# Four extra matmuls with unused results in front of twenty of attention's transpose groups

## The chip, the cores and the metric

The kernel runs on one core of one Trainium2 chip. The metric is the device time of one execution in microseconds (us), from the first to the last instruction with what lies around it. Lower is better. In this document PE is TensorE, DVE is VectorE, ACT is ScalarE, POOL is GpSimd, SP is SyncE.

## What is computed

The reference is a two-layer decoder trunk over 512 tokens of width 1024. Layer 0 is an RWKV-7 mixer, layer 1 is native sparse attention; each stands between two half-step SwiGLU blocks. The change lies in the attention of layer 1, which has 16 heads of width 64 in 4 groups of 4:

```python
lc = jnp.einsum('bqghd,bngd->bqghn', qc, k_cmp) * scale
p_cmp = masked_softmax(lc, ...)                     # 31 compressed keys
o_cmp = jnp.einsum('bqghn,bngd->bqghd', p_cmp, v_cmp)
...
ls = jnp.einsum('bqghd,bqgkd->bqghk', qrc, kg) * scale
p_sel = masked_softmax(ls, causal)
o_sel = jnp.einsum('bqghk,bqgkd->bqghd', p_sel, vg)
...
lw = jnp.einsum('bqghd,bkgd->bqghk', qrc, kw) * scale
p_win = masked_softmax(lw, ...)
o_win = jnp.einsum('bqghk,bkgd->bqghd', p_win, vw)
return gc[..., 0:1] * o_cmp + gc[..., 1:2] * o_sel + gc[..., 2:3] * o_win
```

With 512 tokens, 8 blocks and 16 wanted, all blocks are selected, and the window covers all tokens: both large branches are causal attention over all keys, with different keys and values.

## The kernel before

Attention is a list of 44 steps, `STEPS`, which is run twice (`i` is 0 and 1, two groups of heads in each run, called passes here). Each head has one step `cmp` (the compressed branch, all 512 queries) and four steps `main` (128 queries each, `t` is 0 to 3; the scores of both large branches against the first `128 (t+1)` keys). After every two heads a step `turn` transposes their output; it stands behind `cmp` and `main` `t=0` of the next head. By the number `u` in a pass, the steps `cmp` are 0, 5, 10, 16, 21, 27, 32 and 38, the steps `turn` 12, 23, 34 and 43.

PE works through the list in program order, in three parts for each step, which are staggered: `scores` of step u+1, then `turn(u)` (the method that transposes the probabilities of step u, one 128x128 block at a time, into PSUM banks 4 and 5), then `weigh` of step u-1 (transposed probabilities times values). In the profile `scores` are L2410 (`cmp`) and L2421 to L2423 (`main`), the transposes are L2443 (`cmp`), L2449 (`main`) and L2439 (a step `turn`), and `weigh` is L2468 (`cmp`) and L2475 (`main`; a matmul there shows as two records). DVE takes the negated row maxima (L2592, L2595, L2598), ACT the exponentials (L2506, L2512), and both copy the transposed blocks out of banks 4 and 5 (DVE L2612, ACT L2526 and L2529; for a step `turn` ACT L2524 and then DVE L2607). The methods wait through `at(engine, i, name, u)`, which waits until the event `name` of step u has been counted; `copied_a` and `copied_v` are the copies by ACT and DVE. POOL splits the keys and queries of the next group into a rounded part and a rest meanwhile (L2549 to L2561).

Inputs of the new matmuls are `q2[g]` (queries of a group, 128 columns of the first head as weights) and `khi[g][:, 0]` (512 rounded keys as the moving operand), both already in SBUF.

Of the kernel before, what the change touches and what calls it, by code (L numbers as in the profile page):

```python
# [13 lines left out]
P = 128  # L14
# [679 lines left out]
def recurrence(core, tag, rkv, lora, yhi, ylo):  # L694

    nc, ins = core.nc, core.ins
    with ExitStack() as ctx:
# [109 lines left out]
        def _(pe):  # L807
# [187 lines left out]
            def step(p):  # L995
# [7 lines left out]
                if ahead:  # L1003
                    rates(p + 1)
                product(p, 1)
                turn(p, 0)
                update(p, 1)
                chain(p - 1, 2)
                if ahead:
                    key_norm(p + 1)  # L1010
                product(p, 2)
                turn(p, 1)
                chain(p - 1, 3)
                update(p, 2)
# [5 lines left out]
                chain(p - 1, 4)  # L1020
                update(p, 3)
                turn(p, 2)
                chain(p - 1, 5)
                product(p, 4)
# [724 lines left out]
class SharedKv(Heads):  # L1749
# [129 lines left out]
    def turn(self, pe, n):  # L1879
        u, c = self.turned[n], self.c  # L1880
        pe.wait_ge(self.s["xt"], u + 1)
        for t in range(NT):
            mm = self.core.nc.tensor.transpose(self.p_c[:, t * P:(t + 1) * P], self.xt[:, u % 4, t * P:(t + 1) * P], self.core.ident[:])
        mm.then_inc(c["turned"], 1)
# [422 lines left out]
def attention_steps():  # L2307
    steps, turn = [], None
    for group in range(2):
        for pair in range(2):  # L2310
            for head in range(2):
                steps.append(("cmp", group, pair, head, 0))
                steps += [("main", group, pair, head, t) for t in range(NT)][0:1]
                if turn and head == 0:
                    steps.append(turn)
                steps += [("main", group, pair, head, t) for t in range(1, NT)]
            turn = ("turn", group, pair, 0, 0)
    return steps + [turn]


STEPS = attention_steps()
# [14 lines left out]
class Attend:  # L2336
# [62 lines left out]
    def scores(self, pe, i, u):  # L2399
# [23 lines left out]
            mm = nc.tensor.matmul(bank[:, at0 + b, t * P:n], self.ident16[:], self.causal16[:], start=False, stop=True)  # L2423
        mm.then_inc(s["scores"], 1)

    def turn(self, pe, i, u):
        nc, s, bank = self.nc, self.s, self.bank
        kind, g, pair, head, t = STEPS[u]
        self.at(pe, i, "copied_v", u - 1)
        self.at(pe, i, "copied_a", u - 1)  # L2430
        if i == 0 and u == 0:
            pe.wait_ge(self.heads.s["ln"], ND)
        if i == 0 and u == 1:
            pe.wait_ge(self.heads.s["t2"], ND - 1)
        if kind == "turn":
            last = max(w for w in range(U) if STEPS[w] == ("main", g, pair, 1, NT - 1))
            self.at(pe, i, "o", last)
            for t in range(NT):
                mm = nc.tensor.transpose(bank[:, 4, t * P:(t + 1) * P], self.osb[:, pair, t], self.core.ident[:])  # L2439
        elif kind == "cmp":  # L2440
            self.at(pe, i, "probs", u)
            for t in range(NT):
                mm = nc.tensor.transpose(bank[0:N_CMP, 4, t * P:(t + 1) * P], self.probs[:, u % 2, 0, t * N_CMP:(t + 1) * N_CMP],  # L2443
                                         self.core.ident[:])
        else:
            for b in range(2):
                self.at(pe, i, "probs_sel" if b == 0 else "probs", u)
                for j in range(t + 1):
                    mm = nc.tensor.transpose(bank[:, 4 + b, j * P:(j + 1) * P], self.probs[:, u % 2, b, j * P:(j + 1) * P],  # L2449
                                             self.core.ident[:])  # L2450
        mm.then_inc(s["turned"], 1)
# [302 lines left out]
```

## Time and profile before

| | |
|---|---|
| median of 3 runs | 2480.82 us (2479.68 to 2481.47) |
| the profiled execution, its own time | 2479.42 us |
| its span, first to last instruction | 2477.6 us |
| PE busy | 2356.4 us, 95% of the span |
| mean granted clock of TensorE | 0.974 |
| attention on PE | about 1801 to 2058 us of the span |

A granted clock of 1.00 is 2.4 GHz, 0.50 is 1.2 GHz. Matmuls on PE overlap each other, so what a matmul costs in a dense row of them is read from the distance between two starts and not from its duration: in the rows below the number at the start of a timeline row is its start in us from the beginning of the span, the next its length in us, and a bracket at its end is the time that the engine stood idle before it with what released it.

### The profile page before, as it was taken

How to read it: one execution, taken by the hardware profiler on the slowest of the kernel's cores; microseconds unless marked ns; L12 is line 12 of the kernel's file. 1: busy time of each engine (PE TensorE's matmuls, PEld its weight loads, DVE VectorE, ACT ScalarE, POOL GpSimd, SP SyncE). 2: the span in 40 equal slices, each digit the busy share in tenths (PEclk: the TensorE clock that was granted, in tenths of full speed). 3: DMA queues.
4: the chain of work that ended last, by engine and by line, in shares of the span. 5: the costliest groups of instructions: out<-in, count | busy, mean ns of one | idle time of the engine just before them, and what ended most of it. 6: DMA issues, size and time to landing. Idle time of an engine off the chain costs nothing. (4 is left out here: it accounts for less than half of the span.)

```text
span 2477.6 us, 43846 instructions
## 1 busy us (share of the span) xinstructions
PE 2356.4 (95%) x17558; PEld 1926.6 (78%) x17558; DVE 1536.2 (62%) x2159; ACT 647.8 (26%) x1250; POOL 499.2 (20%) x334
## 2 busy tenths in 40 slices
PE   7999998997988789999999999999999999999999
PEld 6888886784766568888888888888778887888887
DVE  7656467846777556655575565647766666655654
ACT  3101014534555521010023310102544552200001
POOL 3212031002122132121230121213221102212211
PEclk9999998998999989999999999999988999999999
DMA  4333332431111033323265242333300002232322
GB/s 139 102 90 97 102 93 81 143 110 57 30 30 27 3 94 93 102 85 110 79 175 158 86 118 85 101 99 97 86 1 14 14 2 85 85 110 85 104 87 72
DMA packets 371394, 206.54 MB, mean 83 GB/s; under 512 B 18400, under 2 KB 360352, under 8 KB 371232
## 3 DMA queue, kind: packets, MB, share of 16 engines
q1 hardware_dynamic: 364752, 192.11, 27.1%
q10 hardware_dynamic: 6480, 12.13, 1.4%
q8 instruction: 119, 1.95, 0.3%
q14 instruction: 43, 0.35, 0.0%
HBM read 192.61 MB, written 11.60 MB: 82 GB/s over the span
## 5 line engine op out<-in xcount | busy, mean ns | idle before, releaser
L158 PE MATMUL bank_b<-hhi_b,w_hi_b 128*128 128x512 f32 x872 | 345.6, 396 | 0.0
L160 PE MATMUL bank_b<-hhi_b,w_lo_b 128*128 128x512 f32 x872 | 339.5, 389 | 0.0
L159 PE MATMUL bank_b<-hlo_b,w_hi_b 128*128 128x512 f32 x872 | 339.3, 389 | 0.0
L151 DVE TENSOR_TENSOR w_lo_b<-w_raw,w_hi_b 128x1024 fp32r<-128x1024 f32 (+1 forms) x165 | 289.7, 1756 | 5.7
L158 PE MATMUL bank_a<-hhi_a,w_hi_a 128*128 128x512 f32 x480 | 189.2, 394 | 7.7 <-DVE hlo_a L573 7.7
L159 PEld LDWEIGHTS bank_b<-hlo_b,w_hi_b 128*128 128x128 f32 x872 | 163.7, 188 | 37.0 <-issue 3.4
L158 PEld LDWEIGHTS bank_b<-hhi_b,w_hi_b 128*128 128x128 f32 x872 | 163.7, 188 | 36.6 <-issue 3.4
L160 PEld LDWEIGHTS bank_b<-hhi_b,w_lo_b 128*128 128x128 f32 x872 | 163.7, 188 | 34.4
L159 PE MATMUL bank_a<-hlo_a,w_hi_a 128*128 128x512 f32 x480 | 188.4, 392 | 0.0
L160 PE MATMUL bank_a<-hhi_a,w_lo_a 128*128 128x512 f32 x480 | 188.2, 392 | 0.0
L479 POOL TENSOR_TENSOR act_b<-gated_b,usc_b 128x512 f32<-128x512 f32 x44 | 63.9, 1451 | 485.1 <-ACT gated_b L458 485.1
L151 DVE TENSOR_TENSOR w_lo_a<-w_raw,w_hi_a 128x1024 fp32r<-128x1024 f32 (+2 forms) x96 | 158.3, 1648 | 3.3
L458 ACT ACTIVATE gated_b<-gsc_b 128x512 f32<-128x512 f32 x44 | 27.9, 634 | 495.1 <-DVE gsc_b L369 495.1
L369 DVE TENSOR_TENSOR gsc_b<-bank_b,rstd_b 128x512 f32<-128x512 f32 x44 | 30.4, 691 | 193.4 <-PE bank_b L160 193.4
L158 PE MATMUL bank_b<-ahi_b,w_hi_b 128*128 128x512 f32 x352 | 137.4, 390 | 1.2 <-DVE x_res L381 1.2
L158 PE MATMUL bank_c<-hhi_c,w_hi_c 128*128 128x512 f32 x352 | 137.3, 390 | 0.0
L159 PE MATMUL bank_b<-alo_b,w_hi_b 128*128 128x512 f32 x352 | 136.9, 389 | 0.0
L160 PE MATMUL bank_c<-hhi_c,w_lo_c 128*128 128x512 f32 x352 | 136.9, 389 | 0.0
L160 PE MATMUL bank_b<-ahi_b,w_lo_b 128*128 128x512 f32 x352 | 136.9, 389 | 0.0
L159 PE MATMUL bank_c<-hlo_c,w_hi_c 128*128 128x512 f32 x352 | 136.9, 389 | 0.0
L151 DVE TENSOR_TENSOR w_lo_c<-w_raw,w_hi_c 128x1024 fp32r<-128x1024 f32 (+1 forms) x76 | 134.8, 1774 | 2.6
L149 DVE CAST w_hi_b<-w_raw 128x1024 fp32r<-128x1024 f32 (+1 forms) x165 | 112.5, 682 | 4.3 <-PEq L2195 4.3
(373 smaller groups left out, 4914.5 us busy)
## 6 DMA issues: line engine op xcount, KB each, us to landing
w_raw<-in_ffn_w_gate_dram SPq DMA_DIRECT2D x88, 512.0 KB, 3.8
w_raw<-in_ffn_w_up_dram SPq DMA_DIRECT2D x88, 512.0 KB, 3.8
w_raw<-in_ffn_w_down_dram SPq DMA_DIRECT2D x64, 512.0 KB, 3.7
w_raw<-in_ffn_w_down_dram SPq DMA_DIRECT2D x32, 384.0 KB, 3.3
w_raw<-in_rw_w_rkv_dram SPq DMA_DIRECT2D x24, 512.0 KB, 3.8
w_raw<-in_kv_w_dram SPq DMA_DIRECT2D x12, 512.0 KB, 4.8
w_raw<-in_rw_w_o_dram SPq DMA_DIRECT2D x8, 512.0 KB, 5.0
w_raw<-in_nsa_w_q_dram SPq DMA_DIRECT2D x8, 512.0 KB, 3.8
```

Source lines behind the costliest of these rows:

```text
L149: nc.vector.tensor_copy(hi, raw).then_inc(s["w_hi"], 1)
L151: nc.vector.tensor_tensor(lo, raw, fp(hi), ALU.subtract).then_inc(s["w_ready"], 1)
L158: nc.tensor.matmul(out, whi, hi, start=first, stop=False)
L159: nc.tensor.matmul(out, whi, lo, start=False, stop=False)
L160: return nc.tensor.matmul(out, wlo, hi, start=False, stop=last)
L369: V.tensor_tensor(region.gsc[:, j], bank[:, j], region.rstd[:], ALU.mult).then_inc(s["gate"], 1)
L458: A(region.gated[:], region.gsc[:, j], ACT.Silu).then_inc(s["silu"], 1)
L479: G_.tensor_tensor(region.act32[:], region.gated[:], region.usc[:, j], ALU.mult).then_inc(s["act32"], 1)
```

## The change

In front of the transposes of step u, a new method issues four matmuls into PSUM bank 5: for every step `cmp` but the first of a pass, and for each step `main` that stands right behind a step `turn`. Nothing reads their results; the next transposes into bank 5 overwrite them. Ahead of them PE waits for the ACT copy out of bank 5 of the step before (or, behind a turn, of the one before that).

```diff
+    def keep_clock(self, pe, i, u):
+
+        kind, g = STEPS[u][:2]
+        if u and (kind == "cmp" or kind == "main" and STEPS[u - 1][0] == "turn"):
+            self.at(pe, i, "copied_a", u - 1 if kind == "cmp" else u - 2)
+            for _ in range(4):
+                self.nc.tensor.matmul(self.bank[:, 5], self.q2[g][:, 0, 0:P], self.khi[g][:, 0], start=True, stop=True)
+
     def turn(self, pe, i, u):
         nc, s, bank = self.nc, self.s, self.bank
         kind, g, pair, head, t = STEPS[u]
+        self.keep_clock(pe, i, u)
         self.at(pe, i, "copied_v", u - 1)
         self.at(pe, i, "copied_a", u - 1)
```

In each pass the places are the steps `cmp` 5, 10, 16, 21, 27, 32, 38 and the steps `main` 13, 24, 35: ten places, twenty in both passes, 80 matmuls of 128x512.

The first of them on PE, step 5 of the first pass, as a piece of the difference in PE's program order (lines of the kernel after are 9 higher from the method on):

```order
 L2422 MATMUL bank_b<-klo_b,q_b 128x128
 L2423 MATMUL bank_b<-causal_b,ident_b 128x128
-L2443 MATMUL bank_b<-ident,probs_b 31x128 x4
-L2475 MATMUL bank_b<-vv_b,pt_b 128x64 x8
+L2432 MATMUL bank_b<-khi_b,q_b 128x512 x4
+L2452 MATMUL bank_b<-ident,probs_b 31x128 x4
+L2484 MATMUL bank_b<-vv_b,pt_b 128x64 x8
 L2421 MATMUL bank_b<-khi_b,q_b 128x256
 L2422 MATMUL bank_b<-klo_b,q_b 128x256
```

The four new matmuls (L2432) stand between the scores of step 6 and the transposes of step 5; what follows keeps its order.

A place behind a turn, step 13 of the first pass, on PE as well:

```order
 L2422 MATMUL bank_b<-klo_b,q_b 128x384
 L2423 MATMUL bank_b<-causal_b,ident_b 128x128
-L2449 MATMUL bank_b<-ident,probs_b 128x128 x4
+L2432 MATMUL bank_b<-khi_b,q_b 128x512 x4
+L2458 MATMUL bank_b<-ident,probs_b 128x128 x4
 L2421 MATMUL bank_b<-khi_b,q_b 128x512
 L2422 MATMUL bank_b<-klo_b,q_b 128x512
```

Here the four stand between the scores of step 14 and the transposes of step 13, for which PE waits until the output of the turn has been copied out of bank 4.

## Rows read from the trace of the kernel before

**Rows 1.** The page: the span, and busy time of the engines.

```profile
span 2477.6 us, 43846 instructions
PE 2356.4 (95%) x17558; PEld 1926.6 (78%) x17558; DVE 1536.2 (62%) x2159; ACT 647.8 (26%) x1250; POOL 499.2 (20%) x334
```

**Rows 2.** Windows over attention: stretch, its length, busy time of engines, granted clock.

```profile
1801.00:1814.50 13.50, 10.44 (x65) 7.33 (x64) 10.89 (x27) 6.43 (x26) 9.08 (x7) 1.00 0.00 1
1814.50:1838.40 23.90, 23.55 (x103) 21.09 (x103) 10.09 (x36) 7.85 (x30) 3.74 (x4) 0.50 0.00 1
1838.40:1886.20 47.80, 43.53 (x352) 38.79 (x352) 33.63 (x111) 26.12 (x96) 6.49 (x6) 1.00 0.08 18
1886.20:1903.30 17.10, 17.10 (x76) 14.70 (x75) 6.72 (x23) 5.48 (x24) 4.41 (x5) 0.50 0.01 1
1903.30:1940.80 37.50, 34.03 (x278) 30.62 (x277) 23.77 (x82) 18.83 (x66) 0.00 (x0) 1.00 0.04 9
1940.80:1951.00 10.20, 8.90 (x41) 7.38 (x40) 5.08 (x18) 4.51 (x21) 7.40 (x7) 0.50 0.23 51
1951.00:2060.30 109.30, 99.57 (x801) 88.30 (x801) 72.85 (x254) 58.84 (x216) 3.48 (x4) 1.00 0.00 1
2060.30:2067.10 6.80, 5.33 (x13) 4.17 (x14) 6.66 (x8) 0.00 (x0) 0.00 (x0) 0.50 0.55 159
```

**Rows 3.** Timeline of PE: transposes of steps 3, 5 and 10, first pass.

```profile
1814.85 1.51 PE L2449 MATMUL bank_b<-ident,probs_b 128*128 128x128 f32 x6 [2.54 <-ACT pt_b L2529]
...
1825.06 1.06 PE L2443 MATMUL bank_b<-ident,probs_b 128*31 128x128 f32 x4
...
1844.23 0.60 PE L2443 MATMUL bank_b<-ident,probs_b 128*31 128x128 f32 x4
```

**Rows 4.** Timeline of PE, second pass: transposes of steps 3 and 10.

```profile
1952.21 0.83 PE L2449 MATMUL bank_b<-ident,probs_b 128*128 128x128 f32 x6
...
1971.04 0.60 PE L2443 MATMUL bank_b<-ident,probs_b 128*31 128x128 f32 x4
```

**Rows 5.** Timeline of PE, first pass: steps 25, 26 and 32.

```profile
1881.64 0.84 PE L2449 MATMUL bank_b<-ident,probs_b 128*128 128x128 f32 x6 [0.32 <-issue]
...
1885.33 1.15 PE L2449 MATMUL bank_b<-ident,probs_b 128*128 128x128 f32 x8 [1.01 <-ACT pt_b L2529]
...
1909.04 0.60 PE L2443 MATMUL bank_b<-ident,probs_b 128*31 128x128 f32 x4
```

**Rows 6.** Timeline of PE, second pass: steps 25 and 32.

```profile
2008.46 0.84 PE L2449 MATMUL bank_b<-ident,probs_b 128*128 128x128 f32 x6 [0.32 <-issue]
...
2027.04 0.60 PE L2443 MATMUL bank_b<-ident,probs_b 128*31 128x128 f32 x4
```

**Rows 7.** Timeline of PE: a dense row of 128x512 matmuls, full clock.

```profile
1800.12 0.40 PE L158 MATMUL bank_b<-hhi_b,w_hi_b 128*128 128x512 f32 x1
1800.35 0.39 PE L159 MATMUL bank_b<-hlo_b,w_hi_b 128*128 128x512 f32 x1
```

**Rows 8.** Timeline of PE: the same kind of matmul at half clock.

```profile
2063.22 0.63 PE L158 MATMUL bank_c<-ohi_b,w_hi_c 128*128 128x512 f32 x1
2063.64 0.63 PE L159 MATMUL bank_c<-olo_b,w_hi_c 128*128 128x512 f32 x1
```

**Rows 9.** Timeline of PE: 128x512 scores with the operands of the new matmuls.

```profile
2048.54 0.47 PE L2421 MATMUL bank_b<-khi_b,q_b 128*128 128x512 f32 x1
2048.86 0.40 PE L2422 MATMUL bank_b<-klo_b,q_b 128*128 128x512 f32 x1
```

**Rows 10.** Timeline of PE: the wait behind a turn (step 12, second pass).

```profile
1977.05 0.23 PE L2423 MATMUL bank_b<-causal_b,ident_b 128*128 128x128 bf16 x1
1978.34 0.44 PE L2449 MATMUL bank_b<-ident,probs_b 128*128 128x128 f32 x2 [1.06 <-DVE olo_b L2607]
```

**Rows 11.** Timeline of ACT and PE, second pass: ACT's copy of step 15, transposes of step 16.

```profile
1985.11 0.57 ACT L2529 ACTIVATE pt_b<-bank_b 128x512 f32<-128x512 f32 x1
...
1985.88 0.60 PE L2443 MATMUL bank_b<-ident,probs_b 128*31 128x128 f32 x4
```

## The prediction

> **What bounds the kernel now.** I read four views, from coarse to fine. The page comes first: PE is busy for 2356.4 us of the span of 2477.6 us, 95% [rows 1], so what is added on PE in a dense part of the program costs time unless it stands in a gap. The windows over attention are second, cut where the granted clock changes. They show four stretches at 0.50, 1.2 GHz: 23.9, 17.1, 10.2 and 6.8 us long, and 1.00, 2.4 GHz, between them [rows 2]. The first three lie in attention, 51.2 us together; the fourth lies behind it, in the output projection. At half clock PE is busy for 23.55 us of 23.9 and 17.10 of 17.1, while DVE falls from 33.63 us in 47.8 (0.70) to 10.09 in 23.9 (0.42) [rows 2]: there nothing but PE sets the pace. At full clock PE is busy for 99.57 us of 109.3 [rows 2]; the rest is gaps.
>
> The timeline is third; it prices the half clock. The list of steps is the same in both passes, so the same pieces can be compared. From the transposes of step 3 to those of step 10 the first pass takes 1844.23 - 1814.85 = 29.38 us [rows 3], the second, at full clock, 1971.04 - 1952.21 = 18.83 us [rows 4]. The first stretch thus costs 10.55 us for its 23.9 us, 0.44 us for each us at half clock. From step 25 to step 32 it is 1909.04 - 1881.64 = 27.40 us [rows 5] against 2027.04 - 2008.46 = 18.58 us [rows 6], 8.82 us more, of which 1.01 us is a wait for ACT ahead of the transposes of step 26 [rows 5] and 7.8 us the second stretch, 0.46 for each us. The third has no clean counterpart; by 0.45 for each us it costs 10.2 x 0.45 = 4.6 us. All that can be won in attention is therefore 10.6 + 7.8 + 4.6 = 23 us.
>
> **What stands before a fall, and where the clock comes back.** The first fall, at 1814.5, comes at the end of an idle time of 2.54 us ahead of the transposes of step 3 [rows 3], the second, at 1886.2, behind the 1.01 us of rows 5. In the second pass the transposes of step 25 stand at the same place without a fall [rows 2, 6]. The first two stretches end at the same place of the list: 1838.4 is 5.8 us ahead of step 10, 1903.3 is 5.7 us ahead of step 32 [rows 2, 3, 5]. By the program order that is behind the scores of a step with `t=3`, the row of wide matmuls (four of 128x512) that is the densest thing attention has. The clock falls where PE has little to do and returns where wide matmuls stand close together.
>
> **The change, part by part.** It adds 80 matmuls of 128x512 in twenty groups of four, and one wait ahead of each group. DVE, ACT, POOL and SP execute what they did.
>
> Price of a group. A dense row of such matmuls goes at 0.23 us each at full clock [rows 7] and 0.42 us at half clock [rows 8], so a group takes 0.92 us or 1.68 us. With the very operands of the new matmuls, the first one of a pair of scores takes 0.32 us to the next [rows 9], but that one follows a narrow matmul with other weights, so I use it only as the upper bound, 1.28 us a group. The lower bound is nothing, where a gap of PE hides the group. The Trainium skill, page "TensorE: Matmul & The Clock Gate", section "Back-to-back issue gap", gives some 131 ns for each matmul of 512 columns in a sustained stream of loads and matmuls, against about 216 ns for a single one; the row of this case, 230 ns, agrees with the second. By the page's first figure a group would cost 0.52 us.
>
> The six groups behind a turn. PE has issued the scores at 1977.05 and then stands idle for 1.06 us, until DVE's copy L2607 is done, at 1978.34 [rows 10]. The new matmuls wait for a copy two steps back, which is old by then, so they fit in: 0.92 against 1.06 us. Cost 0 (if a group takes 1.28 us, 6 x 0.22 = 1.3 us). Without that cover they would cost 5.5 us.
>
> The fourteen groups in front of a `cmp` step. There the transposes follow the scores with no idle time, both at step 10 [rows 4] and at step 16 [rows 11]: no cover, and what follows on PE moves back by the whole group. The wait that comes with them is free: ACT's copy out of bank 5 ends at 1985.11 + 0.57 = 1985.68, and PE comes to this place at 1985.88 [rows 11]. Queued behind it are the transposes of the step, for which ACT and DVE wait, and these then run later by the same 0.92 us; since PE is the slower side, no gap elsewhere shrinks that I can name. Thirteen at full clock, 12.0 us, and the one of step 5 in the first pass, at half clock, 1.7 us: 13.7 us.
>
> What they give back. The first fall comes at 1814.5, 10.6 us before the first group could run (step 5, at 1825.06) [rows 2, 3]. Nothing in the change prevents it. But the group of step 5 is as dense as the scores of a `t=3` step, and it follows the scores of step 6. I expect the clock back right behind it, at about 1825.1 + 1.7 + 1.5 = 1828.3 instead of 1838.4. That is 10 us fewer at half clock, 10 x 0.44 = 4.4 us. The second fall needs the thin place of steps 25 and 26 and the wait in it, which came once in the two passes. The group ahead of step 24 brings dense work near it, but it stands in front of the scores of 25 and not in the thin place itself, so it is no sure cure. In the likeliest case the second stretch does not open: 7.8 us. If it opens, the group of step 27 ends it some 7 us later, and 10 x 0.45 = 4.5 us are won, with a second group at half clock (0.8 us more). The third stretch opens at the passage between the passes, where steps 39 to 43 and 0 to 4 have no new matmuls; I leave it and the fourth as they are, a gain of 0.
>
> **The sum.** 13.7 - 4.4 - 7.8 = +1.5 us. Against the profiled execution's own 2479.42 us that makes 2480.9; this execution lies 1.4 us under the median of the runs, so on the median it is 2480.8 + 1.5 = 2482.3 us.
>
> **The rivals.**
>
> *The second stretch opens all the same, or one elsewhere instead.* For it: the groups move all that follows by several us, and thin places at `t=2` and `t=3` of each head stay. Cost 13.7 + 0.8 - 4.4 - 4.5 = +5.6 us, 2486.4; with the third stretch longer by 3 to 7 us, up to 2490.
>
> *The clock does not care.* The groups stand at the wrong places or are too short, each stretch ends where it did, and the whole price is left: 14 x 0.92 = 12.9 us, and at half clock for three or four of them 0.8 us more each, +15 to +16 us, 2496. Against it: the stretches do end behind a dense row of about this size. That the change does not do what it says is this case.
>
> *The other side: all later falls stay away.* The mechanism is the passage between the passes: if its fall at 1940.8 is as marginal as that of step 26, a small shift is enough, and 4.6 us come on top, with about 3 us more if the fourth stretch (6.8 us at 0.45) goes too. It decides if both happen: 1.5 - 4.6 - 3.1 = -6.2 us, 2474.6; with the third alone -3.1 us, 2477.7, not to be told from no change. Against it: no new matmul stands between step 38 and step 5 of the next pass, and PE has 1.3 us of idle time in the 10.2 us of the third stretch [rows 2].
>
> *The groups are cheaper than a dense row.* If a group lets DVE and ACT catch up and so closes gaps of PE behind it, or its four matmuls follow each other more closely than 0.23 us because they share their weights, the price halves to 6.9 us: 1.5 - 6.8 = -5.3 us, 2475.5. The rows have no gap for it beside the one behind a turn and a third of a us in front of a `t=2` step [rows 5, 6]. The page's 131 ns would come to about this.
>
> **How the numbers follow.** A measurement of this kernel tells 0.2%, 5.0 us, from no change. Chances: the likeliest case 0.42, with its own range 2478 to 2486 (price of a group up to 1.28 us adds 14 x 0.36 = 5 us; the third stretch gone takes 4.6). The second stretch or another opens, 0.30, of which two thirds end above 2485.8. The clock does not care, 0.08. All later falls stay away or shorten, 0.13, of which half is under 2475.9. Cheaper groups, 0.07. Faster: 0.06 + 0.05 and a little of the first case, 0.14. Slower: 0.20 + 0.08 and 0.04 of the first, 0.32. Within 0.2%: 0.54. The range reaches from the two faster cases to the top of the second rival, 2474 to 2491; outside it are the case in which the clock does not care and the ends of the others.
>
> **What the profile after would show.** The new line L2432 with 80 matmuls, start to start 0.23 us. Idle time of PE ahead of the transposes behind a turn falls from 1.06 to about 0.15 us. In the second pass, from the transposes of step 25 to those of step 32, 18.58 us become 20.4, since the groups of steps 27 and 32 lie between. A first fall at 1814.5 as before, its end at about 1828. The stretch round step 26 gone or at most some 7 us. The third and the fourth about 10 and 7 us. The prediction is wrong if the first stretch still lasts 24 us, if new stretches at half clock open, or if a group takes clearly more or less than 0.92 us.

## The result, and the profile after

| | before | after |
|---|---|---|
| median of 11 runs each | 2479.68 us (2475.72 to 2484.68) | 2485.22 us (2480.98 to 2489.11) |
| the profiled execution, its own time | 2479.42 us | 2484.16 us |
| its span | 2477.6 us | 2482.4 us |

The ratio is 1.0021, with a 95% interval of 1.0011 to 1.0030: the change makes the kernel some 5.5 us slower. Single runs of either kernel lie up to 9 us apart, more than the effect, so it takes medians to see it. One run of the kernel before, among those set beside the later experiments, took 4132.46 us at a mean granted clock of 0.666; no ratio and no range below counts it.

The windows of the kernel after, cut where its granted clock changes, with the columns of [rows 2]:

```profile
1814.60:1828.30 13.70, 13.33 (x59) 12.52 (x60) 6.25 (x19) 4.91 (x20) 3.21 (x4) 0.50 0.00 1
1828.30:1886.30 58.00, 55.63 (x427) 48.19 (x426) 38.12 (x127) 30.14 (x111) 7.08 (x6) 1.00 0.06 15
1886.30:1893.20 6.90, 6.90 (x31) 6.24 (x31) 2.91 (x8) 2.31 (x10) 3.81 (x5) 0.51 0.00 1
1893.20:1940.90 47.70, 43.55 (x337) 37.84 (x336) 29.05 (x102) 23.17 (x85) 0.00 (x0) 1.00 0.06 13
1940.90:1951.20 10.30, 10.26 (x41) 7.88 (x42) 5.50 (x15) 3.87 (x15) 8.51 (x8) 0.50 0.11 24
...
2063.80:2070.60 6.80, 3.06 (x7) 2.51 (x8) 5.66 (x7) 0.23 (x1) 0.00 (x0) 0.50 0.26 77
```

The first stretch at half clock begins where it did, at 1814.6, and lasts 13.7 us instead of 23.9. The second still opens, and lasts 6.9 us instead of 17.1. The third and fourth are as long as before. In attention 51.2 us at half clock have become 30.9.

Where the first stretch ends, PE's timeline of the kernel after shows the group of step 5 at half clock and the scores behind it back at full clock:

```profile
1825.06 0.33 PE L2423 MATMUL bank_b<-causal_b,ident_b 128*128 128x128 bf16 x1
1825.15 2.06 PE L2432 MATMUL bank_b<-khi_b,q_b 128*128 128x512 f32 x4
1827.01 1.05 PE L2452 MATMUL bank_b<-ident,probs_b 128*31 128x128 f32 x4
...
1829.98 0.28 PE L2422 MATMUL bank_b<-klo_b,q_b 128*128 128x256 f32 x1
```

And step 26, the wait in the thin place, with the group of step 27 behind it:

```profile
1884.84 1.06 PE L2458 MATMUL bank_b<-ident,probs_b 128*128 128x128 f32 x8 [1.02 <-ACT pt_b L2538]
...
1888.73 2.06 PE L2432 MATMUL bank_b<-khi_b,q_b 128*128 128x512 f32 x4
1890.59 1.05 PE L2452 MATMUL bank_b<-ident,probs_b 128*31 128x128 f32 x4
```

The wait for ACT is there as before, 1.02 us against 1.01 [rows 5]. A group takes 1827.01 - 1825.15 = 1.86 us at half clock. At full clock, in the second pass, first in front of a `cmp` step and then behind a turn:

```profile
1970.87 0.23 PE L2423 MATMUL bank_b<-causal_b,ident_b 128*128 128x128 bf16 x1
1970.91 1.17 PE L2432 MATMUL bank_b<-khi_b,q_b 128*128 128x512 f32 x4
1971.92 0.60 PE L2452 MATMUL bank_b<-ident,probs_b 128*31 128x128 f32 x4
...
1977.92 0.23 PE L2423 MATMUL bank_b<-causal_b,ident_b 128*128 128x128 bf16 x1
1977.96 1.17 PE L2432 MATMUL bank_b<-khi_b,q_b 128*128 128x512 f32 x4
1979.21 0.66 PE L2458 MATMUL bank_b<-ident,probs_b 128*128 128x128 f32 x4
```

From the last row of the scores (1970.87) to the transposes it is 1.05 us, where the kernel before had 0.07 (1970.97 to 1971.04), so a group costs 0.98 us. Counted in the same way it costs 1.83 us at half clock: 1.95 us (1825.06 to 1827.01), where the kernel before had 0.12 (1824.94 to 1825.06). Behind the turn no idle time is left in brackets, where [rows 10] had 1.06 us, and the transposes come as soon as they did, 1.29 us behind the last row of the scores in both kernels.

The account of attention can be made from the same anchors as before: the transposes of steps 3, 10, 25 and 32 of the first pass, of step 42, and of step 3 of the second pass.

```profile
1814.97 1.51 PE L2458 MATMUL bank_b<-ident,probs_b 128*128 128x128 f32 x6 [3.11 <-ACT pt_b L2538]
...
1841.76 0.60 PE L2452 MATMUL bank_b<-ident,probs_b 128*31 128x128 f32 x4
...
1881.13 0.84 PE L2458 MATMUL bank_b<-ident,probs_b 128*128 128x128 f32 x6 [0.32 <-issue]
...
1905.95 0.60 PE L2452 MATMUL bank_b<-ident,probs_b 128*31 128x128 f32 x4
...
1931.96 1.06 PE L2458 MATMUL bank_b<-ident,probs_b 128*128 128x128 f32 x8 [0.79 <-issue]
...
1951.05 0.89 PE L2458 MATMUL bank_b<-ident,probs_b 128*128 128x128 f32 x6
```

Steps 3 to 10 take 26.79 us instead of 29.38 [rows 3], with two groups in them (1.83 + 0.98), so 5.4 us came back. Steps 25 to 32 take 24.82 us instead of 27.40 [rows 5], again with two groups: 5.4 us. Together that is 10.8 us for 20.4 us less at half clock, 0.53 for each us. The price is 12 x 0.98 + 2 x 1.83 = 15.4 us. The difference is +4.6 us. From step 42 to step 3 of the second pass it is 19.09 us; before it was 18.13 us, 1.0 us more at an equally long stretch, with no group in it. Why is not shown. These are the anchors of the kernel before in that piece, the last turn and step 0 of the next pass between them:

```profile
1934.08 0.63 PE L2449 MATMUL bank_b<-ident,probs_b 128*128 128x128 f32 x4 [0.79 <-issue]
...
1939.00 0.63 PE L2439 MATMUL bank_b<-ident,lora_lg 128*128 128x128 f32 x4 [0.79 <-DVE lora_lg L2648]
...
1943.06 1.03 PE L2443 MATMUL bank_b<-ident,probs_b 128*31 128x128 f32 x4 [1.30 <-ACT probs_b L2506]
```

That makes +5.6 us in attention. The projection behind it gives 1.0 us back, since fewer of its matmuls fall into the fourth stretch (they start at 2067.5 and the clock returns at 2070.6; before it was 2061.8 and 2067.1). The span is 4.8 us longer.

### The profile page after: what moved, and what is told of

Read it like the earlier page. It is cut to its first block and busy times, and to the rows that moved or that the text cites. A ratio compares the mean times of both kernels' runs of the same rounds, so it can differ in the third digit from the quotient of the medians.

```text
span 2482.4 us, 44006 instructions
## 1 busy us (share of the span) xinstructions
PE 2367.8 (95%) x17638; PEld 1933.0 (78%) x17638; DVE 1538.9 (62%) x2159; ACT 649.2 (26%) x1250; POOL 499.0 (20%) x334
## 3 DMA queue, kind: packets, MB, share of 16 engines
q8 instruction: 119, 1.95, 0.3%
```

## The experiments

All kernels below compute the same output as the two compared; only the matmuls with unused results differ. Times are medians, each beside the median of the kernel before from runs taken together with it.

**Which groups do what: only those of steps 5 and 27, first pass.**

```diff
-        if u and (kind == "cmp" or kind == "main" and STEPS[u - 1][0] == "turn"):
+        if i == 0 and u in (5, 27):
```

> Only the groups ahead of steps 5 and 27 of the first pass are left, 8 new matmuls. Theory (these two alone shorten the half clock, the others only cost): both stretches end as in the changed kernel, 13.7 and 6.8 us long; won 10.2 x 0.44 + 10.2 x 0.45 = 9.1 us, paid 2 x 1.82 = 3.6 us: 5.5 us under the kernel before, ratio about 0.9978. Rival (the other groups have a part in it, by what they add to the activity of PE between): one of the two stretches is long again, and the time is within 2 us of the kernel before.

Measured: 2473.38 us against 2479.3, ratio 0.9974 (0.9963 to 0.9985), 5.9 us faster. The windows of its trace:

```profile
1815.10:1828.80 13.70, 12.84 (x57) 12.04 (x58) 6.70 (x22) 5.19 (x21) 3.69 (x4) 0.50 0.01 1
...
1883.30:1890.10 6.80, 6.80 (x31) 6.14 (x30) 2.18 (x8) 2.61 (x13) 4.68 (x5) 0.50 0.01 4
```

The two stretches are those of the changed kernel, 13.7 and 6.8 us. Two of the twenty groups are enough for all the shortening; the other eighteen are not needed for it.

**Only the six groups behind a turn.**

```diff
-        if u and (kind == "cmp" or kind == "main" and STEPS[u - 1][0] == "turn"):
+        if u and kind == "main" and STEPS[u - 1][0] == "turn":
```

> Only the six groups behind a turn. Theory (they lie in a wait and change no stretch): time as before within 1 us, the four stretches 23.9, 17.1, 10.2 and 6.8 us, PE's idle time behind a turn about 0.1 us instead of 1.06. Rival A (they cost, by what they delay on other engines): 3 to 6 us slower. Rival B (the group ahead of step 24 has part in shortening the second stretch): that stretch under 14 us and the time 2 us or more under before.

Measured: 2479.63 us against 2479.3, ratio 0.9998 (0.9989 to 1.0008). They cost nothing and bring nothing. In the trace the first two stretches are 23.9 and 17.1 us, the third is 13.6 and not 10.2 us:

```profile
1811.90:1835.80 23.90, 22.69 (x102) 20.65 (x102) 11.18 (x38) 8.72 (x34) 3.92 (x5) 0.50 0.00 1
...
1883.60:1900.70 17.10, 17.10 (x78) 15.42 (x76) 7.49 (x25) 5.78 (x24) 5.00 (x5) 0.50 0.00 0
...
1938.20:1951.80 13.60, 12.71 (x53) 10.08 (x53) 6.20 (x21) 5.49 (x24) 9.22 (x9) 0.50 0.22 55
```

**Only the fourteen groups in front of `cmp` steps.**

```diff
-        if u and (kind == "cmp" or kind == "main" and STEPS[u - 1][0] == "turn"):
+        if u and kind == "cmp":
```

> Only the fourteen groups ahead of cmp steps. Theory: 12 at full clock x 0.98 = 11.8 us and 2 at half clock x 1.82 = 3.6 us, against 9.1 us won: 6 us slower than before in attention, 5 to 6 us in the whole, the same as the changed kernel within 1 us. Rival (the groups behind turns have a part in cost or gain): differs from the changed kernel by 2 us or more.

Measured: 2483.87 us against 2478.86, ratio 1.0024 (1.0013 to 1.0035): 5.0 us slower, as the changed kernel within 1 us. The whole effect is in these fourteen. In the trace the first two stretches are 13.7 and 6.8 us, as in the changed kernel.

**Only the seven groups in front of `cmp` steps of the second pass**, where the clock was whole.

```diff
-        if u and (kind == "cmp" or kind == "main" and STEPS[u - 1][0] == "turn"):
+        if i == 1 and u and kind == "cmp":
```

> Only the seven groups ahead of cmp steps of the second pass, where the clock is whole before the change. Theory (they bring nothing there and each costs 0.98 us): 6.9 us over before, less up to 1 us if the fourth stretch covers less of the projection. Rival (part of the price is got back, since PE's other waits shrink): 3 us or less over before.

Measured: 2485.09 us against 2479.52, ratio 1.0021 (1.0011 to 1.0030), 5.6 us slower. That is 0.80 us a group, against 0.98 less what the fourth stretch gives back (7 x 0.98 - 1.0 = 5.9 us). These seven alone cost as much as the whole change costs on balance. Its profiled run, the fastest of nine, had a second stretch of 3.4 us where nothing had been changed ahead of it: how long a stretch lasts varies from run to run.

**What about a group brings the clock back: narrow matmuls.** As the kernel with two groups, with eight matmuls of 64 columns in each.

```diff
-        if u and (kind == "cmp" or kind == "main" and STEPS[u - 1][0] == "turn"):
+        if i == 0 and u in (5, 27):
-            for _ in range(4):
-                self.nc.tensor.matmul(self.bank[:, 5], self.q2[g][:, 0, 0:P], self.khi[g][:, 0], start=True, stop=True)
+            for _ in range(8):
+                self.nc.tensor.matmul(self.bank[:, 5, 0:64], self.q2[g][:, 0, 0:P], self.khi[g][:, 0, 0:64], start=True, stop=True)
```

> As two_groups, but with eight matmuls of 64 columns in each group instead of four of 512: at half clock a group takes about the same time (8 x 0.22 = 1.8 us), PE is as busy, but 512 columns pass instead of 2048. Theory (the columns count): the stretches are as long as before the change, 23.9 and 17.1 us, and the time is 3 to 4 us over before. Rival (that PE is busy counts): the stretches end as in two_groups, and the time is 5.5 us under before.

Measured: 2483.02 us against 2479.3, ratio 1.0016 (1.0008 to 1.0025), 3.7 us slower. Its timeline and its windows:

```profile
1828.24 1.90 PE L2432 MATMUL bank_b<-khi_b,q_b 128*128 128x64 f32 x8
1829.95 1.04 PE L2452 MATMUL bank_b<-ident,probs_b 128*31 128x128 f32 x4
```

```profile
1816.60:1843.90 27.30, 25.84 (x114) 23.28 (x115) 11.06 (x40) 9.09 (x34) 2.97 (x3) 0.50 0.00 1
...
1891.70:1908.80 17.10, 17.10 (x77) 15.22 (x77) 6.97 (x23) 5.06 (x20) 3.85 (x5) 0.50 0.00 0
```

A narrow group keeps PE busy for 1829.95 - 1828.24 = 1.71 us, nearly as long as a wide one (1.86 us). The stretches last 27.3 and 17.1 us, where the kernel before had 23.9 and 17.1. The price is paid, 2 x 1.71 = 3.4 us, and nothing comes back. So the time for which PE counts as busy does not decide: behind four matmuls of 512 columns the clock came back, behind eight of 64 columns, with twice as many weight loads, it did not.

**Four matmuls in the wait of step 26 alone.** From here on all edits are against the kernel before, and the count, the bank and the step whose use of the bank must be over come from a table. `turn` calls the new method first, as in the changed kernel; that line is left out below.

```diff
+    def keep_clock(self, pe, i, u):
+
+        count, bank, before = {(0, 26): (4, 7, 23)}.get((i, u), (0, 0, 0))
+        g = STEPS[u][1] if STEPS[u][0] != "turn" else 0
+        if count:
+            self.at(pe, i, "o", before)
+            if STEPS[u][0] == "turn":
+                pe.wait_ge(self.s["split"], 15)
+            for _ in range(count):
+                self.nc.tensor.matmul(self.bank[:, bank], self.q2[g][:, 0, 0:P], self.khi[g][:, 0], start=True, stop=True)
```

> One group alone: four matmuls in the wait of 1.01 us ahead of step 26 of the first pass, in the thin place itself (the changed kernel has a group two steps ahead of it, before step 24, and its second stretch opened). Theory: first stretch 23.9 us as before, the second does not open, the third as before; 7.8 us won, 0.1 us paid: 7.5 us under before, ratio about 0.997. Rival (the second stretch was absent in the runs with the waits filled because the first was gone or put off and everything stood elsewhere): the second stretch opens, time as before within 2 us.

Measured: 2472.49 us against 2478.86, ratio 0.9975 (0.9966 to 0.9985), 6.4 us faster. The timeline at the place, and the windows:

```profile
1884.02 1.19 PE L2435 MATMUL bank_b<-khi_b,q_b 128*128 128x512 f32 x4
1885.16 1.06 PE L2461 MATMUL bank_b<-ident,probs_b 128*128 128x128 f32 x8
```

```profile
1813.70:1837.60 23.90, 22.51 (x100) 20.52 (x100) 11.35 (x39) 8.88 (x34) 4.10 (x5) 0.50 0.00 1
1837.60:1933.20 95.60, 88.80 (x713) 78.80 (x712) 64.45 (x217) 50.37 (x184) 10.90 (x10) 1.00 0.06 14
```

The wait is filled and the transposes follow at once. The first stretch is as before, the second is gone. Four matmuls in the wait prevent what the six groups ahead of it in the changed kernel, 24 matmuls, did not. The single trace would not be enough, since the kernel with the seven groups of the second pass shows that this stretch can shorten by itself. But all twelve runs have a mean granted clock of 0.976 to 0.978, where 19 of the 22 runs of the kernel before beside them have 0.972 to 0.975 and only three 0.977.

**Both waits, of steps 3 and 26.** Eight matmuls ahead of step 3 (as a table entry `(0, 3): (8, 6, 0)`) and the four of step 26.

> No group at the places of the change; instead eight matmuls in the idle time of 2.54 us ahead of step 3 and four in that of 1.01 us ahead of step 26, both in the first pass, into the bank that the weighing of the step before overwrites next. Theory (a fall comes of PE having little to do just then, and dense work in that very gap prevents it): the first and the second stretch do not open; 10.6 + 7.8 = 18 us won, nothing paid, ratio about 0.993. Rival A (what matters is the thin work round the gap and not the gap): the stretches open all the same, the time is as before. Rival B (a fall put off comes a little later, since what follows is thin too): stretches of other lengths, 5 to 10 us won.

Measured: 2463.28 us against 2479.3, ratio 0.9936 (0.9922 to 0.9950). Four of the six runs lie between 2460.9 and 2463.3, two at 2469.6 and 2471.7. The profile is of the slowest:

```profile
1815.11 0.85 PE L2458 MATMUL bank_b<-ident,probs_b 128*128 128x128 f32 x6 [1.20 <-ACT pt_b L2538]
```

```profile
1817.30:1837.80 20.50, 20.50 (x92) 18.03 (x91) 7.59 (x28) 5.83 (x25) 0.96 (x1) 0.50 0.00 1
1837.80:1929.90 92.10, 85.58 (x688) 76.12 (x688) 63.10 (x215) 49.77 (x183) 10.91 (x10) 1.00 0.04 10
```

The second stretch is gone, but eight matmuls left 1.20 us of the wait ahead of step 3 idle, and the first stretch opened at 1817.3, a step later, and lasted 20.5 us. The mean granted clock is 0.981 to 0.983 in the four faster runs and 0.978 in the two others, so both of these spent more time at half clock. Theory and rival B both hold, each for some of the runs.

**The same with twelve ahead of step 3 and four ahead of step 4** (`(0, 3): (12, 6, 0), (0, 4): (4, 7, 1)`).

> As in_the_waits, with twelve instead of eight matmuls ahead of step 3 and four more ahead of step 4, where PE has no wait, so that these cost 0.98 us. Theory (the fall that in_the_waits only put off in its profiled run comes in the thin steps 3 and 4): neither the first nor the second stretch opens, in no run; 10.6 + 7.8 - 1.0 = 17.4 us under before, and the single times lie close together. Rival (it is put off once more, or was none of the gap's doing): the times spread as in in_the_waits, over some 10 us.

Measured: 2462.19 us against 2479.52, ratio 0.9929 (0.9916 to 0.9942), 17.3 us faster, five runs within 1.7 us. In its trace neither of the two stretches opens:

```profile
1806.70:1922.70 116.00, 108.68 (x856) 95.53 (x855) 80.73 (x266) 60.70 (x223) 20.11 (x19) 1.00 0.04 9
```

Two things were changed at once here, the longer filling (0.51 us of the wait is left) and the group of step 4; which of them made the runs alike is not separated.

**The passage between the passes and the end of attention.** Three matmuls ahead of steps 42 and 43 of each pass, five ahead of step 0 of the second, eight behind the last transposes.

```diff
+        {(0, 42): (3, 7, 39), (0, 43): (3, 7, 41), (1, 0): (5, 7, -3), (1, 42): (3, 7, 39), (1, 43): (3, 7, 41)}
...
+        if i == 1 and u == U - 1:
+            for _ in range(8):
+                nc.tensor.matmul(bank[:, 5], self.q2[0][:, 0, 0:P], self.khi[0][:, 0], start=True, stop=True)
```

> Only the part of all_waits at the passage between the passes and at the end of attention: three matmuls ahead of steps 42 and 43 of each pass, five ahead of step 0 of the second, eight behind the last transposes. Theory: the third stretch (10.2 us) does not open and the fourth (6.8 us) is gone or shorter; 4.6 + 2.4 us won, 1 us paid: 6 us under before. Rival (the third stretch comes from the thin steps as such, the group is too late or the fourth comes from the wait for DVE behind attention): both stretches as before, time 0 to 1 us over before.

Measured: 2476.52 us against 2479.52, ratio 0.9988 (0.9979 to 0.9997): 3.0 us faster and not 6. The profile is of the slowest of its eleven runs, so only pieces of it are compared here and not its whole. The windows show that the third stretch is gone and the fourth is 3.4 us:

```profile
1908.60:2065.60 157.00, 145.88 (x1145) 127.64 (x1145) 103.64 (x353) 82.18 (x302) 10.91 (x10) 1.00 0.03 7
2065.60:2069.00 3.40, 3.40 (x9) 2.62 (x9) 3.33 (x5) 0.00 (x0) 0.00 (x0) 0.51 0.61 180
```

So the mechanism was right and the value expected was not. The timeline from step 42 to step 3 of the second pass:

```profile
1940.06 1.06 PE L2461 MATMUL bank_b<-ident,probs_b 128*128 128x128 f32 x8
...
1944.98 0.63 PE L2451 MATMUL bank_b<-ident,lora_lg 128*128 128x128 f32 x4
...
1949.04 0.60 PE L2455 MATMUL bank_b<-ident,probs_b 128*31 128x128 f32 x4 [0.47 <-ACT probs_b L2521]
...
1955.43 0.85 PE L2461 MATMUL bank_b<-ident,probs_b 128*128 128x128 f32 x6 [0.53 <-issue]
```

That is 15.37 us against 18.13, a gain of 2.8 us for a stretch of 10.2 us. From the last turn of a pass to step 0 of the next it takes 4.06 us (1944.98 to 1949.04) at full clock with five new matmuls in it, and took 4.06 us before (1939.00 to 1943.06): PE waits for ACT there at either clock, so half the clock cost nothing there. From step 42 to the turn it is 4.92 us in both, three new matmuls included. All of the gain lies behind step 0.

**All waits together.** Both tables in one, with twelve ahead of step 3.

> No group at the places of the change. New matmuls only where PE waits anyway: twelve ahead of step 3 and four ahead of step 26 of the first pass, three ahead of steps 42 and 43 of each pass, five ahead of step 0 of the second pass, eight behind the last transposes of attention. Theory (a fall follows a wait in a thin place, and dense work in the wait prevents it): none of the four stretches opens; 10.6 + 7.8 + 4.6 us and some 2.4 us of the fourth (5.3 us of projection at half clock) won, up to 2 us paid: 23 us under before, ratio about 0.991. Rival (a fall is only put off to the next thin place, as the profiled run with the waits filled had it): one or two stretches are left elsewhere, 10 to 17 us won.

Measured: 2457.27 us against 2479.52, ratio 0.9916 (0.9901 to 0.9930), 22.3 us faster, the best of all kernels here. The windows over attention and the first part of the projection in its trace show no stretch at half clock at all:

```profile
1801.00:1860.00 59.00, 55.93 (x423) 47.67 (x422) 43.02 (x138) 32.01 (x119) 12.74 (x11) 1.00 0.01 1
1860.00:1920.00 60.00, 56.65 (x453) 49.92 (x451) 41.19 (x137) 32.17 (x119) 10.90 (x10) 1.00 0.06 15
1920.00:1980.00 60.00, 57.27 (x453) 50.20 (x453) 40.98 (x140) 34.17 (x131) 10.92 (x10) 1.00 0.06 15
1980.00:2041.00 61.00, 55.07 (x427) 47.68 (x426) 39.67 (x133) 29.69 (x106) 0.00 (x0) 1.00 0.01 1
2041.00:2085.00 44.00, 43.82 (x193) 36.32 (x194) 27.20 (x34) 8.73 (x14) 15.28 (x7) 1.00 0.43 125
```

One of its six runs took 2466.5 us, at a mean granted clock of 0.981, where the other five have 0.984 to 0.986: it spent more time at half clock. Where, no trace shows.

**All waits and step 4.**

> all_waits with four more matmuls ahead of step 4 of the first pass, which stand in no wait and cost 0.98 us. Theory (the one slow run of six in all_waits, 9 us over the others, was a fall put off into the thin steps 3 and 4): no such run, times within 2 us of each other, the median 1 us over that of all_waits or equal, ratio about 0.992. Rival (that run was something else): the spread stays.

Measured: 2458.16 us against 2478.86, ratio 0.9915 (0.9901 to 0.9928), six runs between 2454.5 and 2460.4. No run lies 9 us above the others, but they aren't within 2 us of each other either. With six runs each, whether the group of step 4 removes the one high run of the kernel without it (2466.5 us) stays open. Its trace, of the slowest run, has one stretch of 3.4 us at half clock in the projection, from 2044.6.

## Why the prediction came out as it did

The median is 2485.22 us, in the range of 2474 to 2491, and 2.9 us over the predicted 2482.3. Part of that nearness is luck: the forecast stood on a median of three runs, 2480.82 us, and eleven give 2479.68. The difference, which the mechanism has to explain, was forecast as +1.5 us and is +5.5. The change is slower by just more than what was called no change. The likeliest case was not the one that happened; the first rival was.

- **What bounds it.** Right. Attention is paced by PE, and the account in PE's order closes to the length of the span within 0.2 us.
- **The first stretch.** Right in what brings the clock back and in the size: it was to come back at about 1828.3, and did. To the tenth that was luck: the 1.5 us that the prediction put between the end of the group and the clock's return stood on no row, and they were 1.3 us here (1827.01 to 1828.3) and 2.6 us behind the group of step 27 (1890.59 to 1893.2). The shortening was worth 5.4 us where 4.4 was forecast: each us less at half clock gave back 0.53 us, where the whole stretch had cost 0.44 for each. Why the rates differ is not shown.
- **The second stretch: the step that failed.** "In the likeliest case the second stretch does not open: 7.8 us." It opened at 1886.3, and what came back was 5.4 us and not 7.8, with a second group paid at half clock. The group of step 24 is over before the thin place begins and nothing was put into the wait itself, as the prediction had noted before it chose the other way. The kernel with four matmuls in that wait shows the reason: there the stretch does not open, with the first one as before. Once open, the stretch ended some 7 us later behind the group of step 27, and the rival's 2486.4 us is 1.2 us from the median. It lies so close partly because errors cancel in it: its price of 14.5 us is 0.9 us too low and its gain of 8.9 us is 1.9 us too low.
- **The price of a group.** Mis-sized: 0.98 us, forecast 0.92. The first of four takes 0.32 us to the next, as in [rows 9], and only the other three 0.23. I had that row and took it for a bound. At half clock it is 1.83 us and not 1.68. Over fourteen groups the price is 15.4 us against 13.7: about half of the difference is the second group at half clock, the rest is the size. The sign named for the second pass says the same: from step 25 to step 32 it was 18.58 us and was to be 20.4, and it is 2031.83 - 2011.29 = 20.54 us, 0.98 for each of two groups.

```profile
2011.29 0.84 PE L2458 MATMUL bank_b<-ident,probs_b 128*128 128x128 f32 x6 [0.32 <-issue]
...
2031.83 0.60 PE L2452 MATMUL bank_b<-ident,probs_b 128*31 128x128 f32 x4
```

- **The rival of cheaper groups.** It fell: no group took less than a dense row does. The 131 ns of the Trainium skill, page "TensorE: Matmul & The Clock Gate", section "Back-to-back issue gap", are seen in none of these rows; the lowest distance between two 128x512 matmuls in the dense rows is 0.22 us.
- **The groups behind a turn.** Right, cost 0: the kernel with only these has a ratio of 0.9998.
- **The third stretch.** Unchanged as forecast. Its value was given as 4.6 us, by the rate of the other two; taking it away brought 2.8 us. The rates of two pieces that PE bounds were carried to a place where PE waits for ACT during part of the stretch. This value stood only in a rival and not in the sum.
- **The other side.** Its chance of 0.13 was small with reason: no group of the change stands where, by the experiments, it would prevent a fall.

## What to carry to other kernels

Work whose only purpose is to hold TensorE's clock belongs into the waits that stand before the falls; here it cost nothing there and prevented them, in most runs. In front of work that bounds the time each group is paid in full, and here twelve of fourteen were paid for a clock that was whole. Find the falls in the trace first, and value each stretch by comparing the same program piece at both clocks, since a stretch in which PE waits for another engine is worth less. Take wide matmuls: behind the narrow ones the clock did not come back, though they kept PE busy for nearly as long. Whether narrow ones in the waits would prevent a fall was not tried.

## What the runs showed of the hardware

The clock fell to 1.2 GHz though PE was busy for 237.1 of the 257 us of attention (92%) in the kernel before. One fall came behind a wait of only 1.01 us, with transposes and matmuls of 64 and 31 columns round it. In the second pass the transposes of step 25 and 26 came without that wait, and the clock stayed whole. With four 128x512 matmuls in the wait it stayed whole in the first pass too. The length of a wait alone does not decide: the 1.06 us behind the turn of [rows 10], with rows of wide scores on both sides, was followed by no fall.

The same program doesn't fall in the same way in each run. The kernel before took between 2469.2 and 2485.3 us beside the experiments, and in one run of a kernel with a partly filled wait the stretch opened one step later instead of not at all. In three of the thirteen traces (the kernel with narrow matmuls, that of the passage, and that of both waits and step 4) a further stretch of 3.4 us opened at the start of attention, ahead of everything changed, behind a wait of 0.6 us for DVE; the kernel before has the same wait, 0.61 us, and its clock stayed whole there. A fraction of a per cent between two such kernels can't be told from single profiles.
